# One decoder layer on one NeuronCore: token sums of the seven-product stage made in place on fp32 values that co leaves, stripe loads moved ahead of returning rows, sample scores written in place

## The reference

```
h = RMSNorm(x);  [q|f|i|g|u] = h @ w_in
A = HGRN2 recurrence over 4 heads of q, f, i, per-head RMSNorm, gate sigmoid(g)
B = trailing means of u over 2/4/8/16 tokens minus u, per-group map, per-channel scale
x = x + concat(A, B) @ w_out
x = x + CrossAttn(RMSNorm(x), memory K/V)          (4 heads of 256, 256 memory tokens)
a, b = split(RMSNorm(x) @ w_ffn_in);  x = x + (silu(a) * b) @ w_ffn_out     (width 2816)
y = RMSNorm(x)
```

## Time and profile before

| | |
|---|---|
| median of 3 runs | 1523.63 us (1523.59 to 1524.26) |
| the profiled execution | 1524.86 us |
| its span (first to last instruction) | 1523.0 us |
| mean granted TensorE clock | 0.984 of full |
| TensorE busy | 1462.2 us, 96% |
| VectorE, ScalarE, GpSimd busy | 920.0, 404.2, 633.7 us |
| DMA | 124.46 MB, mean 82 GB/s |

### The profile page before, as it was taken

One profiled execution on the slowest core, in us unless ns is written; L12 is line 12 of the kernel. 1 busy time (PEld: TensorE's weight loads), 2 busy tenths in 40 slices (PEclk: granted clock), 3 DMA queues, 4 the chain that ended last, 5 costly groups with the idle time before them and its releaser, 6 DMA issues.

```text
span 1523.0 us, 26089 instructions
## 1 busy us (share of the span) xinstructions
PE 1462.2 (96%) x10159; PEld 1419.9 (93%) x10159; DVE 920.0 (60%) x1452; ACT 404.2 (27%) x604; POOL 633.7 (42%) x471
## 2 busy tenths in 40 slices
PE   7999999999999999999987999999999999999998
PEld 7998998979999988779977999999999899999998
DVE  5224478668744277647887667667766758533334
ACT  4021334361020134321023222323232223312011
POOL 2122146135541062115593677777778610000163
PEclk9999999999999999999988999999999999999999
DMA  5311300101151266221121222222122142441113
GB/s 161 111 42 42 97 29 16 55 22 42 42 166 42 79 191 228 83 100 53 42 56 56 70 84 83 73 79 82 60 79 83 56 143 66 165 140 56 42 42 112
DMA packets 161489, 124.46 MB, mean 82 GB/s; under 512 B 10340, under 2 KB 148580, under 8 KB 161411
## 3 DMA queue, kind: packets, MB, share of 16 engines
q1 hardware_dynamic: 161419, 123.49, 26.0%
HBM read 103.12 MB, written 20.58 MB: 81 GB/s over the span
## 4 chain that ended last, share of the span: by engine, by line
PE 64%; POOL 14%; issue 11%; DVE 8%; ACT 2%; SPq 0%; DMA 0%; POOLq 0%; DVEq 0%; ACTq 0%
PE pm L2077 17%; PE pm L2079 17%; PE pm L2078 17%; POOL gb L996 3%; POOL raw L977 2%; POOL raw_c L977 2%; PE pm L2447 2%; PE pm L2374 2%; POOL sum L985 2%; POOL sum L983 2%; PE pm L2472 1%; PE pm L2331 1%; DVE w_lo L1476 1%; PE pm L2333 1%; PE pm L2332 1%
## 5 line engine op out<-in xcount | busy, mean ns | idle before, releaser
L2077 PE MATMUL pm<-x_hi,w_hi 128*128 128x344 f32 x1008 | 330.2, 328 | 18.4 <-DVE w_lo L1476 8.0
L2078 PE MATMUL pm<-x_lo,w_hi 128*128 128x344 f32 x1008 | 325.1, 322 | 0.0
L2079 PE MATMUL pm<-x_hi,w_lo 128*128 128x344 f32 x1008 | 324.9, 322 | 0.0
L1087 ACT ACTIVATE w_hi<-raw 128x1024 fp32r<-128x1024 f32 x90 | 95.4, 1060 | 570.7 <-PE pm L2079 477.4
L2077 PEld LDWEIGHTS pm<-x_hi,w_hi 128*128 128x128 f32 x1008 | 192.4, 191 | 22.7 <-DVE w_lo L1476 8.9
L2078 PEld LDWEIGHTS pm<-x_lo,w_hi 128*128 128x128 f32 x1008 | 192.2, 191 | 0.2
L2079 PEld LDWEIGHTS pm<-x_hi,w_lo 128*128 128x128 f32 x1008 | 192.2, 191 | 0.0
L1476 DVE TENSOR_TENSOR w_lo<-raw,w_hi 128x1024 fp32r<-128x1024 f32 x82 | 121.9, 1486 | 26.8 <-ACT w_hi L1087 26.7
L834 POOL TENSOR_TENSOR raw<-raw,gains 128x1024 f32<-128x1024 f32 x34 | 68.3, 2014 | 125.1 <-DMA raw<-in_w_in 80.9
L914 POOL TENSOR_TENSOR fp<-acc 128x344 f32 (+1 forms) x23 | 22.7, 988 | 212.8 <-DVE acc L2034 205.7
L1926 DVE TENSOR_TENSOR gb<-gb,ga 128x1032 f32<-128x1032 f32 x19 | 53.0, 2787 | 89.9 <-POOL gb L996 89.9
(11 more groups left out here) (357 smaller groups left out, 4051.8 us busy)
## 6 DMA issues: line engine op xcount, KB each, us to landing
raw<-in_w_ffn_in SPq DMA_DIRECT2D x24, 512.0 KB, 4.1
sg_raw<-s_rows SPq DMA_DIRECT2D x22, 516.0 KB, 5.4
s_rows<-gb SPq DMA_DIRECT2D x21, 516.0 KB, 2.7
raw<-in_w_in SPq DMA_DIRECT2D x20, 512.0 KB, 3.8
raw_c<-in_w_ffn_in SPq DMA_DIRECT2D x20, 512.0 KB, 5.1
vc<-in_cache_mem_v SPq DMA_DIRECT2D x16, 512.0 KB, 3.9
xt<-in_x_prompt SPq DMA_DIRECT2D x8, 512.0 KB, 6.1
raw<-in_w_out SPq DMA_DIRECT2D x8, 512.0 KB, 3.9
```

The lines of the kernel that those rows point to most:

```text
L1087: act.activation(w_hi[s][:, :, :], src, ACT.Copy).then_inc(hi_made, 1)
L2077: pe.matmul(out, w_hi[s][:, k, :], hi[:, k, x0:x0 + cols], start=(k == 0), stop=False)
L2078: pe.matmul(out, w_hi[s][:, k, :], lo[:, k, x0:x0 + cols], start=False, stop=False)
L2079: last = pe.matmul(out, w_lo[s][:, k, :], hi[:, k, x0:x0 + cols], start=False, stop=(k == kb - 1))
```

## The change

1. co no longer writes the new x to xnew but to xf, an fp32 tile of 8 x 1032 in the place that tl takes later. VectorE's wait for GpSimd's squares goes, and the loop over pairs is written out. GpSimd squares from xf into a buffer of its own, xsq2.
2. The token sums are four subtractions in place for each half of the channels. Those of half 0 stand in co, behind the last chunks of its stripes 4 to 7; those of half 1 in in_head on VectorE, two ahead of the wait for rb and two behind the first two evictions. GpSimd's are removed. th and tl have the layout of x; ScalarE makes th block by block between the SiLUs of the first block, VectorE tl between its evictions.
3. For the first pair of the sevens sum2 and sum3 have tiles of their own (first2, first3), so that GpSimd's weight sums don't wait for in0's matmuls; they wait for sq_wide. The parts are split in the order 4, 5, 6, 0, 1, 2, 3, most of them inside in0's last stripes, and TensorE's products wait for 4, 5, 6 and 7 parts.
4. In the down phases the stripes of the next pair (of the next phase behind the last) are loaded ahead of the rows; the rows come as NEXT_GROUP has them, one or two for each pair; fb_last is stored behind row 4.
5. The four operations of sample_scores write ssc; ssx and its copy go.

```diff
+        th = put("th", [P, KB, T], F32R, at=r0)
+        tl = put("tl", [P, KB, T], F32R, at=r0 + 18 * Z)
+        xf = put("xf", [P, KB, T], at=r0 + 18 * Z)
+        xsq2 = put("xsq2", [P, 2, CH], at=r2 + Z)
...
+        first2, first3 = (put(f"first{2 + n}", [P, KP, P], at=r2 + Z + 2048 * n)[:, :, :] for n in range(2))
...
+        FIRST_ORDER = (4, 5, 6, 0, 1, 2, 3)
...
                 load_row(0)
                 load_row(1)
+                for s in range(2):
+                    load_stripe(ph["down0"], 0, s)
...
             def load_groups(p):
-                fs = {"down0": (4, 5, 6, 7), "down4": tuple(range(8, 16)), "down8": tuple(range(16, 22)), "down16": ()}[p.name]
-                per = -(-len(fs) // 2)
                 for i in range(p.stripes // 2):
-                    for s in range(2):
-                        load_stripe(p, i, s)
+                    n = (p, i + 1) if i + 1 < p.stripes // 2 else (after.get(p.name), 0)
+                    if n[0]:
+                        for s in range(2):
+                            load_stripe(*n, s)
                     if i == 0 and p.name == "down0":
-                        sp.wait_ge(fprod, 3 * NC)
-                        store_row(FB - 1, 1, fb_last)
                         sp.wait_ge(quad_made, 14 * PAIRS7)
...
-                    if i < 2:
-                        for f in fs[i * per:(i + 1) * per]:
-                            load_row(f)
+                    for f in NEXT_GROUP[p.name][i]:
+                        load_row(f)
+                    if i == 0 and p.name == "down0":
+                        sp.wait_ge(fprod, 3 * NC)
+                        store_row(FB - 1, 1, fb_last)
...
             def in_head(p):
-                pool.wait_ge(stored, 16 * 5)
-                pool.wait_ge(xl_made, 16 * NC)
-                steps = token_sums(pool, t_pool, 0)
-                for n in range(5):
-                    next(steps)
                 for s in range(2):
                     gain_stripe(p, 1, s)
-                for n in steps:
-                    pass
+                pool.wait_ge(sq_wide, 2)
                 weight_sums(0, 0)
...
                 if late(i, par, 1):
                     pool.wait_ge(prod_done, lin(i, par, 14, 8 - 14))
-                else:
-                    pool.wait_ge(mm_done, ph["in0"].done + 6 * HEAD)
...
-                    if i == 0:
-                        token_hi(1)
-                        token_hi(0)
-                for n in range(7):
+                        if i == 0:
+                            for k in ((0, 1), (2, 3), (4, 5, 6, 7))[c]:
+                                token_hi(k)
+                        if (i, c) == (HEAD - 1, 0):
+                            for n in (4, 5, 6):
+                                weight_hi(0, 0, n)
+                for n in range(4):
                     weight_hi(0, 0, n)
...
+            def token_sum(n, step):
+
+                even, odd = slice(4 * n, 4 * n + 4, 2), slice(4 * n + 1, 4 * n + 4, 2)
+                h0, h1 = slice(0, HALF), slice(HALF, T)
+                b11, b12, b21, b22 = xf[:, even, h0], xf[:, even, h1], xf[:, odd, h0], xf[:, odd, h1]
+                out, a, b = ((b11, b12, b11), (b12, b22, b12), (b22, b22, b11), (b21, b21, b22))[step]
+                if step == 0:
+                    dve.wait_ge(sq_made, 8 * NC + 12 * (n + 1) + 2)
+                else:
+                    dve.wait_ge(t_dve, OLD + 4 * n + step)
+                dve.tensor_tensor(out, a, b, ALU.subtract).then_inc(t_dve, 1)
...
+                            if c == 2 and p.name == "co" and i >= 2:
+                                token_sum(0, 2 * (i - 2) + s)
...
                     last = dve.tensor_tensor_reduce(kk, kk, wide((2, 6)[i % 2])[:, h * XD:(h + 1) * XD], 1.0, 0.0,
-                                                    ALU.mult, ALU.add, ssx[:, s, h:h + 1])
-                last.then_inc(ssx_made, 1)
-                dve.wait_ge(ssx_made, 2 * i + s + 1)
-                dve.tensor_scalar(ssc[:, s, i * H:(i + 1) * H], ssx[:, s, :], 1.0, None, ALU.mult).then_inc(ssc_made, 1)
+                                                    ALU.mult, ALU.add, ssc[:, s, i * H + h:i * H + h + 1])
+                last.then_inc(ssc_made, 1)
...
             def in_head(p):
                 split_lo((p, 0, 1))
-                steps = token_sums(dve, t_dve, 1)
-                for n in range(3):
-                    next(steps)
+                token_sum(1, 0)
+                token_sum(1, 1)
                 dve.wait_ge(rb_made, 5)
...
+                    if (i, s) == (0, 0) and c < 2:
+                        token_sum(1, 2 + c)
+                    for k in {(0, 0, 2): (0, 1), (0, 1, 0): (2,), (0, 1, 1): (3,), (1, 0, 0): (4,), (1, 0, 1): (5, 6),
+                              (1, 0, 2): (7,)}.get((i, s, c), ()):
+                        token_lo(k)
+                    for n in {(1, 1, 0): (4, 5, 6), (1, 1, 1): (0, 1)}.get((i, s, c), ()):
+                        weight_lo(0, 0, n)
                 classical(p, ga, gb, 0, between)
-                for n in range(7):
+                for n in range(2, 4):
                     weight_lo(0, 0, n)
```

More of the change, by code:

```diff
@@ L389, in hybrid_layer @@
         sq_w = sem("sq_w")
-        ssx_made = sem("ssx_made")
         ssc_made = sem("ssc_made")
@@ L1341, in silu_chunk, with token_hi @@
                 act.activation(cc, cc, ACT.Silu).then_inc(silu_made, 1)
-            def token_hi(n):
-                for q in range(4):
-                    act.wait_ge((t_pool, t_dve)[n], OLD + 8)
-                    act.activation(th[n][:, :, q, :], tlf[n][:, :, q, :], ACT.Copy).then_inc(th_made, 1)
+            def token_hi(k):
+                act.wait_ge(t_dve, OLD + 4 * (k // 4) + 4)
+                act.wait_ge(mm_done, ph["in0"].done)
+                act.activation(th[:, k, :], xf[:, k, :], ACT.Copy).then_inc(th_made, 1)
             def weight_hi(i, par, n):
@@ L1732, in body @@
                                     split_lo(n)
-                pairs(dve, p, body)
+                            if c == 2 and p.name == "co" and i >= 2:
+                                token_sum(0, 2 * (i - 2) + s)
+                if p.name == "out":
+                    pairs(dve, p, body)
+                else:
+                    dve.wait_ge(stored, 16 * 5)
+                    for i in range(p.stripes // 2):
+                        body(i, i == p.stripes // 2 - 1)
             def queries(p):
@@ L1912, in between @@
                         split_lo(nxt(p, i, s, False))
-                    if i == 0 and 3 * s + c < 5:
-                        next(steps)
-                    if i == 1:
-                        for n, q in (((1, 0), (1, 1)), ((1, 2), (1, 3)), (), ((0, 0), (0, 1)), ((0, 2), (0, 3)), ())[3 * s + c]:
-                            token_lo(n, q)
+                    if (i, s) == (0, 0) and c < 2:
[5 more added lines that the diff above has]
+                        weight_lo(0, 0, n)
                 classical(p, ga, gb, 0, between)
-                for n in range(7):
+                for n in range(2, 4):
                     weight_lo(0, 0, n)
@@ L1952, in seven @@
                     dve.wait_ge(fprod, NC * HEAD)
+                    dve.wait_ge(wl7_made, 7)
                 if end:
```

77 lines of the change are left out of this document (24 added, 53 removed).

## The result

The changed kernel takes 1499.29 us (median of 4 runs, 1499.12 to 1499.78) beside 1523.66 us for the kernel before (4 runs, 1523.59 to 1524.26): a ratio of 0.984, 95% interval 0.9823 to 0.9857, 24.4 us less. The forecast was 1502.3 with a range of 1496 to 1509.

A forecast was written before the change was run, and what follows sets the result against it. TensorE, busy 96%, was taken as the bound, with time to gain only in its waits and lower-clock stretches. Token sums 18.7, scores 2.6 and loads 0 gave 21.3 us off: 1503.6 profiled, 1502.3 median, range 1496 to 1509.

The forecast's parts named there:

- What the stretch could give: In0 and the start of the sevens: 16.4 us of waiting plus 6.7 of lower clock, at most 23.1.
- The wait of 6.3: TensorE's 6.3 us wait for in0's first eviction, held by three token sums on VectorE, would go.
- The new stall: In0, third stripe's weight split: ready 793.0, wanted 790.3, so a 2.7 us stall plus 1.7 at lower clock.
- The alternation: A VectorE operation with inputs in SBUF sits out GpSimd's running one, then the two engines alternate.
- The weight parts: First weight halves of the sevens ready at about 814, TensorE there at about 817: no stall.
- The scores: Dropping the scores' copy ends three TensorE waits: 2.6 us, bounds 1.3 and 3.7; weight splits next, about even.
- The loads: Stripes ahead of rows in the down phases: worth 0, bounds +0.5 and -3.
- Row 15's spare time: Down phases: row 15 lands at 1342.5, is converted in 1.0, wanted 1.2 after 1343.61, leaving 1.3 us.
- late rows: Rival, down phases: returning rows land too late at eight places, 1529.5 us; chance 0.05.
- No new stall: Rival: raw_c's loads land after 783, so GpSimd falls behind in0's third-stripe split; 1497.9 us, chance 0.22.
- VectorE becomes the bound: Rival, in0: stall grows to 4.2 and a second comes at the first seven product; 1507.0 us, chance 0.21.
- The head does not gain: Rival: the norm chain holds in0's first eviction, so only later stalls go; 1512 to 1520 us, chance 0.05.

The follow-up runs named there:

- the control: The changed kernel built and run once more with no edit: 1499.68 us, ratio 0.9837.
- e6: Changed kernel with GpSimd waiting before the raw_c scalings until VectorE has split in0's third stripe: 1496.88 us, ratio 0.9819.
- e3: Changed kernel with the four half-0 token sums moved from co to the head of VectorE's in0 work: 1508.48 us, ratio 0.9889.
- E10: Changed kernel with five additions of 128x1032, useless for the outputs, put on GpSimd at the head of in0: 1509.99 us, ratio 0.9903.
- e4: Changed kernel with the first pair's weight sums waiting for in0's matmuls again and parts split in order 0 to 6: 1504.16 us, ratio 0.9866.
- e2: Changed kernel with the old load order in the down phases, rows ahead of the next pair's stripes: 1499.43 us, ratio 0.9838.
- e1: Changed kernel with the scores' copy from ssx to ssc put back: 1503.68 us, ratio 0.9869.
- e7: Changed kernel with returning rows loaded and split one pair of stripes earlier in down0 and down4: 1493.85 us, ratio 0.9797.
- e5: Changed kernel with VectorE splitting in0's third-stripe weights ahead of the first two token splits: 1501.15 us, ratio 0.9836.
- e8: Changed kernel with the tail's two weight splits behind the last sevens pair's first two pairs of PSUM sums: 1493.95 us, ratio 0.9802.
- e9: Changed kernel with GpSimd's added wait in in0, rows a pair earlier and the tail's splits later, all together: 1488.07 us, ratio 0.9758.

## Why the prediction was right, and what it mis-sized

Set against the profiled execution, the forecast was 1503.6 us and the run after took 1499.3. Of the 4.3 us between them the table accounts for 4.1: 3.3 in the token sums and the weight parts (22.0 in place of 18.7), 1.5 from the drop of the clock that stayed away ahead of down8, less 0.3 in the scores and 0.4 at the start. The 1.5 is chance and no merit of the edit: the control, the same kernel, had the drop. The 3.3 are 1.1 for a stall shorter than forecast, 1.7 for the clock stretch that did not follow it, and 0.5 that the stretch gave beyond its ceiling.

**What the stretch could give** was put at 23.1 us, "at most". It is about right, a little low: in0 and the head of the sevens gave 20.3 + 1.7 = 22.0, and 1.6 of stall is left; 23.6 in all. In e6, with no wait left there, in0 gives 22.2, with the 1.7 at the sevens 23.9.

**The wait of 6.3** went for the reason given. The first eviction came at 775.37 (forecast near 775, scores included), and e3 brings wait and clock stretch back by moving four sums. That sums in co cost nothing was right: e3's cq to co is the same length without them. How the 22 us divide between VectorE's four sums fewer and GpSimd's eight that are gone, no run shows in full. E10, with five additions back on GpSimd, costs 9.5, e3 6.9 and e4 3.8, and each was measured with the other parts in place.

**The new stall** is the mis-sized term, twice. The step "It ends at 777.6 + 15.4 = 793.0", wanted at 790.3, "So I expect one new stall of 2.7 us", had the right instruction and the right place: the only wait left in the stretch is for this split. From the first eviction to the split's end the trace has 14.2 us (775.37 to 789.59) where the step had 15.4. Its VectorE share was too low: it left out three of the four evictions, and took 0.5 for a product that took 1.06. Its GpSimd share was too high, 8.2. What the sum, the token splits, the product and the weight split take beyond their 1.22, 2.36, 0.5 and 1.22 is 1.6 + 3.0 + 0.6 + 1.1 = 6.3, since GpSimd also works beside evictions, which keep their 0.50. The forecast allowed for that in a rival and forgot it here. Too little on one engine and too much on the other nearly cancel, so that the count came within 1.2 us is in part luck. TensorE wanted the split at 788.0 (forecast 790.3, less 2.6 for the scores 787.7). So the stall was 1.6 (0.7 in e2). The other half is the 1.7 us for a stretch at the lower clock behind it: there was none, 1.00 in the row above. The step took it from the stalls of the earlier trace rows, which were 3.5 and longer.

**The alternation** on which that count rests is shown by three runs. With GpSimd held back (e6) the pair of token splits takes 2.36 in place of 5.35; with GpSimd busy (e10) a sum takes 3.4 again. The Trainium skill, SBUF — State Buffer (Who interferes with whom), says that whoever has the shared port pair keeps it for the whole instruction; by that rule the 3.0 us more would be the rest of the scaling that runs and the whole next one, at 1.90 each between 1.9 and 3.8, and the trace agrees.

**The weight parts** ahead of the sevens: no stall, as forecast. e4 shows what they were worth, 3.5 + 1.7, and that they pay for it with the new stall.

**The scores** were put at 2.6, with "about even" for the weight splits as what is late next. e1 measures 2.3: the waits for GpSimd's w_lo, 1.4 us in four where before has 0.8 in one, are that next thing, and it came out slightly to the worse side. Inside the bounds of 1.3 and 3.7.

**The loads** were put at 0, and e2 shows 0. Row 15's spare time was put at 1.3 us. After, its hi part ends at 1320.35 (the row below: ScalarE, the idle time and its releaser in brackets) and VectorE takes it up at 1319.81 + 2.37/2, near 1321.0 (second row):

```profile
1319.29 1.06 ACT L1376 ACTIVATE x_hi<-sg_raw 128x1032 fp32r<-128x1032 f32 x1 [0.39 <-DMA sg_raw<-s_rows]
...
1319.81 2.37 DVE L1966 TENSOR_TENSOR x_lo<-sg_raw,x_hi 128x1032 fp32r<-128x1032 f32 x2
```

That leaves 0.6. The reading that late rows would cost nothing was right with half the spare time it claimed. What it missed is that the stalls in those phases could be ended at all: it called the order behind the last eviction "an order that stays" and asked only whether the new loads hurt. e7 shows 5.9 us there.

**The rivals.** "No new stall" described the mechanism wrongly for this kernel: raw_c's loads were in time. Its price was near all the same, 1497.9 against 1499.3, and e6, which makes its condition true, ran at 1496.9. "VectorE becomes the bound" did not come: one stall, and the weight halves for the sevens in time. E10 shows that five more operations on GpSimd bring it, with stalls of 4.2 and 3.7 at the first eviction and the third stripe, though none at the sevens. "The head does not gain" is refuted by the eviction at 775.37, "late rows" by e2.

## What to carry to other kernels

Before moving work off an engine that is no bound, look at the instructions of the other engine that sit between its own: here the same VectorE split took 1.2 us or 2.3 to 2.7 by whether GpSimd had an operation ready, and one wait put on GpSimd (e6, 1.9 us, no stall left) did what a reordering on VectorE (e5) did only in part. The largest gains came from changing what stands in front of an eviction or a split that TensorE waits for, and the way to find them is the list of TensorE's waits with, for each, the instructions queued ahead of the releaser; three edits of a few lines to such queues (e6, e7, e8) brought 11 us more. Measure parts of a change by the lengths between fixed matmuls of one execution, which mostly repeat to 0.1 us, when medians move by 1 to 2 us from causes outside the edit.

## What the runs showed of the hardware

**The drop of the clock behind a stall is not certain.** Three stalls stand in most kernels here with the same wait. Behind the 3.1 to 3.2 us near the end of the sevens the granted clock fell in ten of eleven profiles, not in e6. Behind the stall ahead of down4 (2.3) it fell in nine of eleven, not in e2 and e8; behind that ahead of down8 (2.9 to 3.1) in eight of eleven, not in after, e4 and e10, and for twice as long in e1 and e5. Waits of 1.6 and less in in0 had no drop in any profile; those of 3.5 to 6.3 in in0 and at the head of the sevens (before, e3, e4, e10) all had one. A drop behind the stalls of 2.3 to 4.2 us costs 1.4 to 1.8 us, as much as a small edit brings, and 2.7 where it is twice as long; behind the 6.3 of before and of e3 it was 3.0 and 2.4. What decides it at 2.3 to 3.2 us is open.

**The start-up varies.** The first norm sum in cq started between 437.3 and 441.3 us in kernels that do the same work up to there. TensorE's waits at the very beginning differ in name more than in length: after has 6.2 us for the loads of x_prompt, before has 1.5 for them and 4.5 for GpSimd. The clock from 118 to 124 us is 0.72 in after and 1.00 in the control, and from 10 to 26 us it is 1.00 and 0.68. No experiment was made on it.

**The interleaving of two engines differs by one instruction** between executions of the same code: in0 took 41.4 in after, the control and e7, and 40.5 in e2. It is one token sum: the row below is e2, where after has 2.80 us at 777.36 and everything behind it comes later. In after GpSimd's scaling of in0's last stripe starts at 777.17, as soon as the stripe's load is there and 0.2 us ahead of that sum; in e2 it starts at 777.41, behind it. In the nine profiles in which the scaling starts 0.1 to 0.3 us ahead of the sum (after, the control, e1, e4 to e9) the sum takes 2.70 to 2.89.

```profile
777.33 1.22 DVE L1691 TENSOR_TENSOR xf<-xf 128x1032 f32<-128x1032 f32 x1
```
